# 256-token FFN parts take the high and low halves of their input as one 512-column operand, and FFN weight slabs come in one transfer each

## The reference

```
def swiglu(h, w_in, w_out):
    gate, up = jnp.split(h @ w_in, 2, axis=-1)
    return (jax.nn.silu(gate) * up) @ w_out

def conv_ffn(h, w_up, conv_w, conv_b, w_down):
    u = dwconv3(h @ w_up, conv_w, conv_b)      # x[t-1]*w0 + x[t]*w1 + x[t+1]*w2 + b
    a, b = jnp.split(u, 2, axis=-1)
    return (jax.nn.silu(a) * b) @ w_down
```

## Time and profile before

| | us |
|---|---|
| median of 3 runs | 3587.77 |
| lowest and highest | 3579.93 and 3588.99 |
| the profiled execution | 3600.29 |
| its span, first to last instruction | 3598.4 |
| PE busy in the span | 3460.6 |
| PE weight loads busy | 2908.5 |
| DVE busy | 2141.9 |
| ACT busy | 1406.6 |
| granted TensorE clock, mean | 0.973 |

### The profile page before, as it was taken

One profiled execution on the slowest core, in us unless ns is written; L12 is line 12 of the kernel. 1 busy time (PEld: TensorE's weight loads), 2 busy tenths in 40 slices (PEclk: granted clock), 3 DMA queues, 4 the chain that ended last, 5 costly groups with the idle time before them and its releaser, 6 DMA issues.

```text
span 3598.4 us, 58200 instructions
## 1 busy us (share of the span) xinstructions
PE 3460.6 (96%) x25380; PEld 2908.5 (81%) x25380; DVE 2141.9 (60%) x3256; ACT 1406.6 (39%) x2252; POOL 170.9 (5%) x306
## 2 busy tenths in 40 slices
PE   9999999999999999999979999999999999999898
PEld 7877885798787788778749987768887887779897
DVE  5764454787567635675565554553568854465674
ACT  4223434665322323222445542453353334344553
POOL 0110000000011000111000000110001100020000
PEclk9999997899999999999989999999999999999999
DMA  7664120000256534665434542212236633234453
GB/s 255 226 194 143 51 88 30 3 4 4 83 187 205 176 99 146 218 215 131 126 115 154 178 135 71 71 59 71 94 112 198 204 119 105 94 106 141 152 177 106
DMA packets 271278, 453.67 MB, mean 126 GB/s; under 512 B 15696, under 2 KB 159184, under 8 KB 269360
## 3 DMA queue, kind: packets, MB, share of 16 engines
q1 hardware_dynamic: 237264, 332.62, 28.5%
q0 software_dynamic: 33760, 117.34, 10.6%
HBM read 447.24 MB, written 1.94 MB: 125 GB/s over the span
## 4 chain that ended last, share of the span: by engine, by line
PE 85%; DVE 8%; ACT 3%; DMA 3%; issue 1%; SPq 0%; DVEq 0%; ACTq 0%
PE bank L1230 83%; DVE WR L2155 2%; DVE W L2164 2%; ACT W L1771 1%; PE bank L1505 1%; ACT WR L1771 1%; DMA ring<-in_w_ada 1%; DVE W L2155 1%; DMA ring<-in_ffn_out 1%; DVE HL L2155 0%; DVE X L2164 0%; DVE small L2495 0%; DMA ring<-in_odd_w_in 0%; DMA W<-in_m 0%; DVE W L2159 0%
## 5 line engine op out<-in xcount | busy, mean ns | idle before, releaser
L1230 PE MATMUL bank<-HH,WR 128*128 128x512 f32 (+1 forms) x9312 | 2430.5, 347 | 51.0 <-DVE HL L2155 29.7
L1230 PEld LDWEIGHTS bank<-HH,WR 128*128 128x128 f32 x9312 | 1642.0, 192 | 296.7 <-DVE HL L2155 39.2
L1230 PE MATMUL bank<-HL,WR 128*128 128x512 f32 (+1 forms) x4656 | 1600.6, 344 | 0.0
L1230 PEld LDWEIGHTS bank<-HL,WR 128*128 128x128 f32 x4656 | 894.3, 192 | 97.1
L2155 DVE TENSOR_TENSOR WR<-ring,WR 128x2048 fp32r<-128x2048 f32 (+3 forms) x300 | 673.2, 2249 | 481.8 <-ACT WR L1771 481.0
L1771 ACT ACTIVATE WR<-ring 128x2048 fp32r<-128x2048 f32 (+3 forms) x300 | 561.4, 1879 | 694.9 <-PE bank L1230 595.2
L1771 ACT ACTIVATE W<-bank 64x256 f32<-64x256 f32 (+4 forms) x586 | 272.9, 474 | 691.4 <-PE bank L1230 649.0
L2164 DVE SCALAR_TENSOR_TENSOR W<-ring,vec,W 128x1024 f32<-128x1024 f32 x308 | 381.8, 1279 | 96.1 <-DMA ring<-in_w_mod 71.8
L1230 PE MATMUL bank<-W 64*64 64x64 f32 (+5 forms) x4030 | 291.8, 270 | 28.1 <-ACT W L1771 25.7
L1230 PEld LDWEIGHTS bank<-W 64*64 64x64 f32 (+3 forms) x4030 | 202.8, 146 | 100.9 <-ACT W L1771 46.0
L1771 ACT ACTIVATE W<-bank,small 128x512 f32<-128x512 f32 (+2 forms) x183 | 113.0, 621 | 220.3 <-DVE small L2495 152.9
(11 more groups left out here) (121 smaller groups left out, 2277.1 us busy)
## 6 DMA issues: line engine op xcount, KB each, us to landing
ring<-in_ffn_in SPq DMA_DIRECT2D x176, 512.0 KB, 5.0
ring<-in_w_mod POOLq DMA_DIRECT2D x128, 512.0 KB, 4.5
ring<-in_w_in SPq DMA_DIRECT2D x52, 1024.0 KB, 5.1
ring<-in_ffn_out SPq DMA_DIRECT2D x176, 256.0 KB, 3.8
ring<-in_w_up SPq DMA_DIRECT2D x88, 512.0 KB, 4.9
ring<-in_w_ada POOLq DMA_DIRECT2D x80, 512.0 KB, 4.7
ring<-in_w_down SPq DMA_DIRECT2D x88, 256.0 KB, 3.5
W<-in_m SPq DMA_DIRECT2D x4, 2048.0 KB, 15.0
```

Of the source, the lines that this page charges most:

```text
L1230: return e.matmul(o, l, r, start=start, stop=stop, skip_group_check=True)
```

## The change

Three edits.

In the 256-token jobs, `HH` and `HL` become the two planes of one tensor `HHL`, so that high and low halves of an activation tile can be read as one operand of 2 x 256 columns. A triple then is two matmuls (`three_wide`): the high weights by both halves into all 512 columns of the bank, and the low weights by the high half into the first 256. `wide` says where: all of `ffn_in`, all but the last slab of `deep`, and the tiles m < 2 of `conv`. In the 512-token jobs nothing changes on PE.

A wide tile leaves two sums in its bank, and these must be added. In `ffn_in` and `conv` ACT copies the second half of the bank to SBUF, and DVE adds the first half to it; the SiLU, the product, or ACT's and DVE's convolution steps then read the sum in SBUF. In `deep` a new step `ev_low` adds the second half, times the gate, to `X` after the last wide slab. The last slab's matmuls of a tile wait for it.

The slabs of all six FFNs are laid out in advance in HBM as they stand in the ring (8 KB for each partition), and each comes in a single DMA of 1 MB.

```
+            def wide(self, m, i):
+                if self.ntok != 256:
+                    return False
+                return self.kind == "ffn_in" or self.kind == "deep" and i < KF // 2 - 1 or self.kind == "conv" and m < 2
...
+                    if k0 + 4 == KF and ntok < NT:
+                        ORDER.append(("ev_low", J, m))
...
+            def both(a, b):
+                return bass.AP(a.tensor, a.offset, [a.ap[0], [b.offset - a.offset, 2], *a.ap[1:]])
+            def three_wide(o, l, r, first, last):
+                mm(o.rearrange("p (h n) -> p h n", h=2), l[0], both(*r), first, False)
+                return mm(o[:, 0:256], l[1], r[0], False, last)
...
+                if J.kind == "deep" and J.ntok < NT and not wide:
+                    q.wait_ge(DVES, ("x_low", J.name, m))
...
+            def silu_wide(J, j):
+                q.wait_ge(DVES, ("ab", J.name, j, 0))
+                act(SG[j % 4][:, 0:256], SG[j % 4][:, 256:512], ACT.Silu, ("sg", J.name, j))
...
+                    act(SG[j % 4][:, 256:512], banks[BANK.get(key, 0)][:, 256:512], ACT.Copy, ("low", J.name, j, b))
+                    if m in (1, 2):
+                        silu_wide(J, 2 * g + m - 1)
...
+                    if J.wide(m, 0):
+                        act(CV[i][:, 256:512], banks[BANK.get(key, 0)][:, 256:512], ACT.Copy, ("low", J.name, g, m))
+                        q.wait_ge(DVES, ("whole", J.name, g, m))
+                        bank = CV[i][:, 256:512]
                     act(CV[i][:, 0:n], bank, ACT.Identity, ("cv", J.name, g, m), scale=Vc(f"cw{l}1", j), bias=Vc(f"cb{l}", j))
...
+                    if J.wide(m, 0):
+                        t = CV[i][:, 256:512]
+                        q.wait_ge(ACTS, ("low", J.name, g, m))
+                        tt(t, t, bank, ALU.add, ("whole", J.name, g, m))
+                        bank = t
...
+            def ev_low(J, m):
+                q.wait_ge(MM, ("low", J.name, m))
+                stt(x, held(key)[:, 256:512], MODS[J.kw["mod"]][:, J.kw["idx"] * 8 + m, 0:1], x, ALU.mult, ALU.add,
+                    ("x_low", J.name, m))
...
+                    if c0 is None:
+                        e.dma_start(ring[i].rearrange("p k c -> p (k c)"), w).then_inc(RING[i].sem, RING[i].mark(("raw", s), by=16))
+                        continue
```

More of the change, by code:

```diff
@@ L325, in lin @@
                             runs.append([c, P, m * P])
-                    s = slab([(wt[k0 * P:(k0 + kc) * P, c:c + w], 0, o) for c, w, o in runs], kc, P * len(cols))
+                    whole = kind in ("ffn_in", "conv")
+                    s = slab([(wt[g, k0 // 4], 0, None)] if whole else
+                             [(wt[k0 * P:(k0 + kc) * P, c:c + w], 0, o) for c, w, o in runs], kc, P * len(cols))
                     J.slabs.append((s, g, k0, kc))
@@ L368, in lin_deep @@
             for k0 in range(0, KF, 2):
-                s = slab([(wt[(k0 + q) * P:(k0 + q + 1) * P, 512 * h:512 * h + 512], 2 * q + h, 0)
-                          for q in range(2) for h in range(2)], 4, 512)
+                s = slab([(wt[k0 // 2], 0, None)], 4, 512)
                 J.slabs.append((s, 0, k0, 2))
@@ L1241, in slab_ @@
                 o = banks[BANK[key]][:, 0:J.ntok]
+                wide = J.wide(m, i)
+                low_done = J.kind == "deep" and J.ntok < NT and i == KF // 2 - 2
+                if J.kind == "deep" and J.ntok < NT and not wide:
+                    q.wait_ge(DVES, ("x_low", J.name, m))
                 for k in range(kc):
@@ L1254, in slab_ @@
                         terms = ((l[0], r[0]), (l[0], r[1]), (l[1], r[0]))
-                    mm(o, *terms[0], first, False)
-                    mm(o, *terms[1], False, False)
-                    t = mm(o, *terms[2], False, last)
+                    if wide:
+                        t = three_wide(banks[BANK[key]], l, r, first, last)
+                    else:
+                        mm(o, *terms[0], first, False)
+                        mm(o, *terms[1], False, False)
+                        t = mm(o, *terms[2], False, last)
                     end = m == len(cols) - 1 and k == kc - 1
-                    if last and end:
+                    if low_done and k == kc - 1:
+                        t.then_inc(MM.sem, MM.mark(("low", J.name, m), *((("used", s),) if end else ())))
+                    elif last and end:
                         t.then_inc(MM.sem, MM.mark(key, ("used", s)))
@@ L2340, in ev @@
                 bank = held(key)[:, 0:n]
-                if J.kind == "tm":
+                if J.kind == "ffn_in" and J.wide(m, 0):
+                    j, b = 2 * g + m % 2, m // 2
+                    t = SG[j % 4][:, 256:512]
+                    q.wait_ge(MM, key)
+                    q.wait_ge(ACTS, ("low", J.name, j, b))
+                    tt(t, t, bank, ALU.add, ("ab", J.name, j, b), ("free", key))
+                    if b:
+                        own()
+                        if j >= 18 and FREED[1] is not None:
+                            q.wait_ge(MM, FREED[1])
+                        tt(G[:, j, 0:n], SG[j % 4][:, 0:n], t, ALU.mult, ("g", J.name, j))
+                elif J.kind == "tm":
                     q.wait_ge(MM, key)
@@ L2392, in ev @@
                     q.wait_ge(MM, key)
+                    if J.kind == "deep" and n < NT:
+                        q.wait_ge(DVES, ("x_low", J.name, m))
                     for h, (a, z) in enumerate(HALVES):
```

39 lines of the change are left out of this document (28 added, 11 removed).

## The result

| | before | changed |
|---|---|---|
| median, first comparison (10 runs each) | 3588.65 us | 3599.07 us |
| lowest and highest | 3579.93, 3598.28 | 3591.02, 3609.46 |
| profiled execution, its span | 3600.29, 3598.4 us | 3609.46, 3607.0 us |
| PE busy, DVE busy, ACT busy | 3460.6, 2141.9, 1406.6 | 3454.2, 2173.3, 1431.8 |

The ratio is 1.0026, with a 95% interval from 1.0014 to 1.0038: the change costs some 9 us, where 6 us of gain were forecast. The time lies above the predicted range, and the sign is wrong.

The account below looks back on a forecast made before the run. The prediction took PE, busy for 96% of the span, as the bound. Its terms, -13.1 + 0.4 + 8.6 - 2.0 = -6.1 us, took the median from 3587.8 to 3581.7 us; range 3571 to 3594.

Parts of the forecast that it names:

- Matmuls, -13.1: Outside `c1`'s first part, 653 wide triples each take 0.34 us instead of 0.36, saving 0.02 each: -13.1 us.
- The two-piece operand: Rival: an operand in two pieces costs as much as two, losing the 13.1 us: 3594.8; chance 0.14 with another pace law.
- The rival of a small fixed time: PE's matmuls cost columns plus 0.0025 us; 653 triples save 1.6 us: 3593.2; chance 0.14 shared with the two-piece operand.
- Added work in `11`, +0.4: In `11`, ACT's copies and DVE's additions are hidden by idle time except behind group 0: +0.4 us (0 to 1).
- the tight place behind group 0: In `11`, four evictions stand before the splits and take some 1.4 us longer; priced at +0.4 us (0 to 1).
- `c1`'s first part, +8.6: Two round trips of 1.06 us a group lengthen DVE's cycle to 12.2 us; PE waits: +8.6 us (+4 to +13).
- the growth in group 1: At the start of `c1`'s first part, two more round trips lengthen PE's 3.02 us wait by 1.6 us.
- the debt: In `c1`'s first part, DVE falls behind PE by 1.0 us a group, using up a 4.7 us reserve.
- The rival of an absorbed debt: In `c1`'s first part DVE's cycle stays at 11.2 us or less: -3.3 instead of +8.6, 3569.8 us; chance 0.18.
- the slower one: Rival: in `c1`'s first part round trips cost 1.5 us, DVE's cycle is 13.1, time 3593.1 us; chance 0.13.
- Transfers, -2.0: FFN slabs land some 0.3 us sooner and share queues less with POOL's rows: -2.0 us (0 to -5).
- The passages: PE's waits at 291 and 1227 us, 4.45 and 3.85 us before, were to shrink by 0.4 us each.

Follow-up runs that it names:

- no_sums: Changed kernel without the second sum of each wide tile in the first parts of `11` and `c1`: ratio 0.9983 to the kernel before.
- one_piece: Changed kernel whose wide matmuls in both parts of `c1` read one contiguous piece of 512 columns: ratio 1.0018 to the kernel before.
- changed_again: The changed kernel, unaltered, timed and profiled once more: 3600.50 us, ratio 1.0032 to the kernel before.
- context_ahead: Changed kernel with `11`'s context norm issued one step ahead, `c1`'s first part narrow, slab transfers of before: ratio 0.9981 to the kernel before.
- both_reordered: Changed kernel, transfers of before, context norm one step ahead, `c1`'s shifted products and SiLU one tile later: ratio 0.9988 to the kernel before.
- transfers_alone: Kernel before with only the new slab layout and single 1 MB transfers, all triples three matmuls: ratio 1.0012 to the kernel before.

## Why the prediction was wrong

**Matmuls, -13.1: a term of the wrong size.** The price of 0.34 a pair came from one spot in the earlier trace rows, the passage between two rows of matmuls. Alternating pairs start 0.347 or 0.353 us apart. The lower value equals the sum of 0.227 and 0.12 that the prediction had named (a saving of 0.013) and put aside. That the sum fits is partly luck: in the records of such a row it is 0.230 to 0.233 from the 512-column matmul to the next start and 0.112 to 0.118 from the 256-column one. With 0.013 in the second parts and 0.007 in the first of `11` (2.4 us for 343 triples, `no_sums`), the 653 triples gain 310 x 0.013 + 343 x 0.007 = 6.4 us, and some 1 us less when the second part of `11` runs at the slower pace. The two-piece operand, a rival, is refuted by `one_piece`. The rival of a small fixed time falls too, since it put a pair 0.0025 us under the 0.36, and pairs gain 0.007 to 0.013. The Trainium skill, "TensorE: Matmul & The Clock Gate", section "Back-to-back issue gap", gives a law for a matmul alone; an estimate by it is 0.216 + 0.109 = 0.325 us for a pair. The trace doesn't agree: its pairs start 0.347 us apart or more.

**Added work in `11`, +0.4: the step that failed.** "Hidden by idle time" was read from busy sums, 46 and 49 of 95 us. The idle time was there, but not free: it was each engine waiting for the other in a closed ring that was only just as long as PE's group. The additions cost 136.43 to 137.96 less 130.55 us, so 6 to 7 us, against a predicted 0 to 1 (in part through the clock: in `changed_again` PE stood at 1.2 GHz for 3.7 us more of the part than in `no_sums`). Of these some 1.2 are the tight place behind group 0 that was seen (PE waits 1.24 us at 1945.21); the rest goes with the ring, since `context_ahead` has all the additions and only 1.1 us over `no_sums`.

**`c1`'s first part, +8.6: right in mechanism and size.** Measured +8.2, with the cycle of 12.2 us, a round trip of 1.09 us (3506.64 to 3507.73) against 1.06, the wait of 9.57 us and the growth in group 1 (1.9 against 1.6) as forecast. PE's group was 11.4 and not 11.2 us, so the debt grew by 0.8 a group and not by 1.0. And PE waited for `WR` in the last three groups alone, not after about three: at the start of group 3 its `rest` still ended 3.6 us before PE came for it (3421.04 against an estimated 3424.7, five groups of 11.41 us before the end of group 7), and 0.8 a group uses that up by group 8. Most of the debt shows as the longer wait before the second part. The rival of an absorbed debt is out, by a wait of 9.57 us; the slower one is too, since its cycle of 13.1 us did not come. The new reading is that this debt was in the order: at 12.2 us the cycle has 2.3 us of stops, 1.3 of them new, and without them `both_reordered` has none of it.

**Transfers, -2.0: nothing.** A 1 MB slab of `ffn_in` lands 5.5 us behind its issue, where two issues took 0.4 + 5.0, and one of `ffn_out` 4.9, where four took 1.4 + 3.8; so one is no sooner and the other 0.3. The passages wait 4.82 and 4.67 us in the first profile, not less than the earlier trace rows; in `transfers_alone` they wait 4.20 and 3.21, in `changed_again` 4.83 and 3.68, so they differ from profile to profile by more than the 0.4 us that the term gave each.

By the measured sizes the sum is -6.4 + 6.5 + 8.2 + 0 = +8.3 us. The first comparison shows 0.26% (0.14 to 0.38), 9.3 us, which holds it. Against the forecast of -6.1 the error is 15.4 us: 6.7 the price of a pair, 6.1 the additions in `11`, 2 the transfers, -0.4 `c1`'s first part, and some 1.0 left over. The first two errors weigh about the same, and neither alone gives the measured time.

## What to carry to other kernels

Before work is called hidden by an engine's idle time, see what ends each idle stretch: if two engines release each other in turn, add up the ring between two passes and compare it with the pace of the bound engine. A 60% busy engine in such a ring has no room. And where a producer's result goes through another engine, issue the consumer's step one tile later: that won back 13 us here at equal clock (16 by the medians) without taking out an instruction.

Take the price of a mixed sequence from a place where that mix goes on, not from a single passage.

## What the runs showed that was not expected

Alternating 512 and 256 columns keep one of two paces in a row that nothing interrupts, 0.347 or 0.353 us a pair, with the same instructions and at full granted clock. Where the clock stayed up almost throughout, the second part of `11` took 62.45 us in three kernels and 63.50 or 63.51 in four others. At the slower pace it is 232 to 242 ns from a 512-column matmul to the next start, at the faster one 230 to 233. Neither the operand's pieces nor the transfers separate the two, and not even the kernel does: the changed kernel ran this part at 0.347 in its first profile and at 0.353 in `changed_again`. In the first part of `11` both paces occur in one profile. What sets the pace stays open.

The granted clock makes most of the scatter of this kernel: at equal clock the runs of one kernel scatter by 2.7 us, without it by 3 to 7. With the clocks laid beside the times, effects of 3.5 us could be told apart that the plain ratios left unclear.
